# A block on one NeuronCore: the feed-forward's first product by seven block products instead of eight

## The reference, cut to what matters

```
mixed = concatenate([y_att, y_conv, y_ssd]) @ w_out            # 1024 x 1024
x = x + rms_norm_2(mixed, norm_mix_post)
h = rms_norm_2(x, norm_ffn_pre)
u = causal_dwconv(h @ ffn_w_up, ffn_conv_w) + ffn_conv_b        # 1024 x 5632, 3 taps
gate, up = split(u, 2)
x = x + rms_norm_2((silu(gate) * up) @ ffn_w_down, norm_ffn_post)
```

## Time and profile before

| | us |
|---|---|
| median of 3 runs | 3002.9 (3000.08 to 3009.09) |
| the profiled execution: its own time | 2991.82 |
| its span, first to last instruction | 2990.1 |
| PE busy | 2783.6 (93%) |
| DVE busy | 1764.5 (59%) |
| ACT busy | 1327.3 (44%) |
| POOL busy | 440.8 (15%) |
| mean granted TensorE clock | 0.968 |

### The profile page before, as it was taken

One profiled execution on the slowest core, in us unless ns is written; L12 is line 12 of the kernel. 1 busy time (PEld: TensorE's weight loads), 2 busy tenths in 40 slices (PEclk: granted clock), 3 DMA queues, 4 the chain that ended last, 5 costly groups with the idle time before them and its releaser, 6 DMA issues. The chain is left out here.

```text
span 2990.1 us, 39148 instructions
## 1 busy us (share of the span) xinstructions
PE 2783.6 (93%) x14736; PEld 2305.0 (77%) x14737; DVE 1764.5 (59%) x2288; ACT 1327.3 (44%) x1890; POOL 440.8 (15%) x389
## 2 busy tenths in 40 slices
PE   8999888989879699999996998879999999999998
PEld 7988677777768588888885876656788888888887
DVE  4441167777764599999996733856664343334313
ACT  5111255555542288787775432344553232332212
POOL 0000055554630110000001500310000000000000
PEclk9999998999989699999998999999999999999999
DMA  6446311011026399999996311010031111110114
GB/s 206 181 166 243 114 37 35 35 36 39 30 89 219 120 386 408 409 411 407 411 410 227 138 42 28 1 58 1 21 108 50 49 49 49 49 47 31 50 50 155
DMA packets 159479, 418.27 MB, mean 140 GB/s; under 512 B 21196, under 2 KB 101120, under 8 KB 146048
## 3 DMA queue, kind: packets, MB, share of 16 engines
q1 hardware_dynamic: 144752, 362.63, 32.6%
q0 software_dynamic: 8848, 33.03, 2.8%
q10 hardware_dynamic: 5760, 20.97, 1.7%
HBM read 347.92 MB, written 68.69 MB: 139 GB/s over the span
## 5 line engine op out<-in xcount | busy, mean ns | idle before, releaser
L3676 DVE SCALAR_TENSOR_TENSOR ffn_acc<-psum,ffn_taps,ffn_acc 128x1023 f32<-128x1023 f32 x88 | 112.8, 1282 | 275.7 <-ACT ffn_acc L3580 269.8
L134 PE MATMUL psum<-part,ffn_w_high 128*128 128x512 f32 x704 | 274.1, 389 | 0.7 <-DVE low L3662 0.7
L136 PE MATMUL psum<-part,ffn_w_low 128*128 128x512 f32 x704 | 273.9, 389 | 0.0
L135 PE MATMUL psum<-low,ffn_w_high 128*128 128x512 f32 x704 | 273.9, 389 | 0.0
L134 PE MATMUL psum<-part,expert_x_high 128*128 128x512 f32 x520 | 207.5, 399 | 2.9 <-issue 1.5
L136 PE MATMUL psum<-part,expert_x_low 128*128 128x512 f32 x520 | 203.7, 392 | 0.0
L134 PE MATMUL psum<-project_w_high,high 128*128 128x448 f32 (+1 forms) x512 | 194.8, 381 | 3.5 <-DVE low L398 3.5
L3580 ACT ACTIVATE ffn_acc<-psum,ffn_taps 128x1024 f32<-128x1024 f32 x44 | 53.1, 1207 | 323.2 <-PE psum L136 323.2
L135 PE MATMUL psum<-project_w_low,high 128*128 128x448 f32 (+1 forms) x512 | 193.9, 379 | 0.0
L136 PE MATMUL psum<-project_w_high,low 128*128 128x448 f32 (+1 forms) x512 | 193.8, 379 | 0.0
L129 DVE TENSOR_TENSOR expert_down_low<-expert_down,expert_down_high 128x2048 fp32r<-128x2048 f32 x62 | 139.3, 2288 | 39.6 <-ACT expert_down_high L124 39.6
(11 more groups left out here) (634 smaller groups left out, 6905.6 us busy)
## 6 DMA issues: line engine op xcount, KB each, us to landing
expert_gate<-in_w_gate_dram SPq DMA_DIRECT2D x32, 2048.0 KB
expert_up<-in_w_up_dram SPq DMA_DIRECT2D x32, 2048.0 KB, 10.0
expert_down<-in_w_down_dram SPq DMA_DIRECT2D x32, 2048.0 KB, 10.9
ffn_w<-in_ffn_w_up_dram SPq DMA_DIRECT2D x44, 512.0 KB, 3.7
y_rows<-expert_y ACTq DMA_DIRECT2D x32, 512.0 KB, 10.9
down_w<-in_ffn_w_down_dram SPq DMA_DIRECT2D x39, 256.0 KB, 2.5
project_w<-in_w_in_dram SPq DMA_DIRECT2D x4, 2048.0 KB, 11.7
mix_ret_in<-ret_feat SPq DMA_DIRECT2D x8, 1024.0 KB, 4.7
```

Source lines behind the costliest of these rows:

```text
L134: pe.matmul(out, left[0], right[0], start=start, stop=False)
L135: pe.matmul(out, left[0], right[1], start=False, stop=False)
L136: return pe.matmul(out, left[1], right[0], start=False, stop=stop)
L3676: v.scalar_tensor_tensor(out=acc[c][u][:, i:], in0=wide(psum, 4 * u + 2 * c, 2)[:, 0:S - i], scalar=taps[:, last_tap - i, ds(at, 1)], in1= ...
```

## The change

A product of 2 x 2 blocks is made with seven block products and fifteen block sums (Winograd's form) instead of eight block products. The blocks: A is the transposed weights (two feature tiles m of 128 by two halves of 512 of the width: A11, A12 of the first tile, A21, A22 of the second), B the features (two halves of the width by two halves of 512 tokens). Sums of A (S1 to S4) are made by DVE for every turn and each of gate and up, sums of B (T1 to T4) once. The seven products, their names in the code, and the PSUM bank of the four that c has: `first` A11·B11 (bank 0), `sixth` S2·T2 (1), `fifth` S1·T1 (2), `seventh` S3·T3 (3), then `third` S4·B22 (2), `fourth` A22·T4 (3), `second` A12·B21 (0). Banks 2, 3 and 0 are used twice, so DVE or ACT must have read them between: `third` waits for `u4`, `fourth` for `c22_u3`, `second` for ACT's copy of the first product (`first_copied`). `first` waits for the low part of A11 and A12 (`low_a1`), `sixth` for that of the sums (`low_sums`).

DVE's seven sums after the products are `u2`, `u4`, `c22_u3` (two), `c12`, `c21`, `c11`; their result `u` stands in SBUF, and the taps (`convolve`) read it there. `u` is one buffer for both c. `hidden` no longer fits into SBUF: each turn's two tiles are stored to DRAM and loaded again for the second product. The out-projection keeps two x tiles instead of four, its last tile interleaves the two halves (so that the transpose of tile 6 stands after 24 of its 48 matmuls), and its tail makes the T sums. Turn 0's products are written out, gate and up alternating, each waiting for its own T; turn 1 and the last are written out as well.

```diff
+            def load_after(j, c):
+
+                sp.wait_ge(made4[c], j * 2 + 2)
+                load_half(j * 2 * P + 2 * P, c, 1, second_loaded)
+                sp.wait_ge(made1[c], j * 2 + 2)
+                load_half(j * 2 * P + 2 * P, c, 0, first_loaded)
...
+            load_after(0, 0)
+            with sp.Fori(0, TURNS - 2) as j:
+                load_after(j, 1)
+                store_hidden(j)
+                load_after(j + 1, 0)
...
+            def multiply(c, b, left, right, made):
+                weights, features = room.left(c, left), room.right(right)
+                for k in range(HALF):
+                    last = three_passes(pe, bank[4 * c + b][:], [w[:, k, :] for w in weights], [f[:, k, :] for f in features],
+                                        start=(k == 0), stop=(k == HALF - 1))
+                last.then_inc(made[c], 1)
...
+            def third(j, c):
+                pe.wait_ge(combined[c], j * COMBINED + 2)
+                multiply(c, 2, "s4", "b22", made3)
+
+            def fourth(j, c):
+                pe.wait_ge(combined[c], j * COMBINED + 4)
+                multiply(c, 3, "a22", "t4", made4)
...
+            for k in range(KT):
+                if k == KT // 2:
+                    turn(TT - 2)
+                for n in range(halves):
+                    out_product(TT - 1, n, k)
...
-            step(0, 1)
-            with pe.Fori(1, TURNS) as j:
-                for u in range(2):
-                    step(j, u)
+                pe.wait_ge(combined[c], j * COMBINED)
+                first(j, c)
+                sixth(j, c)
+                fifth(j, c)
+                seventh(j, c)
+                third(j, c)
+                fourth(j, c)
+                second(j, c)
+
+            with pe.Fori(1, TURNS) as j:
+                for c in range(2):
+                    whole(j, c)
...
+                v.wait_ge(second_loaded[c], j * 16 + 16)
+                v.tensor_tensor(s1, a21, a22, ALU.add).then_inc(summed[c], 1)
+                v.wait_ge(first_loaded[c], j * 16 + 16)
+                v.wait_ge(summed[c], j * SUMS + 1)
+                v.tensor_tensor(s2, s1, a11, ALU.subtract).then_inc(summed[c], 1)
+                v.tensor_tensor(a21, a21, a11, ALU.subtract).then_inc(summed[c], 1)
+                v.wait_ge(summed[c], j * SUMS + 2)
+                v.tensor_tensor(s4, a12, s2, ALU.subtract).then_inc(summed[c], 1)
...
+            def gate_turn(j, once=False):
+                if once:
+                    sums(j, 1)
+                else:
+                    convolve(j - 1, 1, 1)
+                    convolve(j - 1, 1, 0)
+                    sums(j, 1)
+                    u2(j, 0, in_u)
+                    u4(j, 0)
+                    c22_u3(j, 0)
+                low_a1(j, 1)
+                low_a2(j, 1)
+                low_sums(j, 1)
+                hide(j - 1)
+                c12(j, 0)
+                c21(j, 0)
+                c11(j, 0, in_u)
+
+            def up_turn(j, last):
+                convolve(j, 0, 1)
+                convolve(j, 0, 0)
+                if not last:
+                    sums(j + 1, 0)
+                u2(j, 1, in_u)
+                u4(j, 1)
+                c22_u3(j, 1)
...
+                    low_a1(j + 1, 0)
+                    low_a2(j + 1, 0)
+                    low_sums(j + 1, 0)
+                c12(j, 1)
+                c21(j, 1)
+                c11(j, 1, in_u)
```

More of the change, by code:

```diff
@@ L3404, in ffn_stage @@
     with Stage(nc, "ffn") as st:
         st.adopt(out_w_loaded)
[L3406 to L3417, removed]
+        down = FfnDown(nc, st, a, bank, room, feat, store_dram, hidden_dram, out)
@@ L3513, in _ @@
                             turn(t - 1)
-                        last = three_passes(pe, out_bank(t, n)[:], (tile(low, t)[:, k, :], tile(high, t)[:, k, :]),
-                                            (half(out_w_high, n)[:, k, :], half(out_w_low, n)[:, k, :]),
-                                            start=(k == 0), stop=(k == KT - 1))
-                    last.then_inc(product, 1)
+                        out_product(t, n, k)
                 if t == 0:
@@ L3583, in gate, with take_second @@
-            def gate(j, u):
-                act.wait_ge(tapped[0][u], j * last_tap + last_tap)
-                act.activation(acc[0][u][:], acc[0][u][:], ACT.Silu).then_inc(silu_ready[u], 1)
+            def take_second(t):
+                act.wait_ge(turned, t + 1)
+                raw = late_raw if t == TT - 1 else tile(low_raw, t)[:, HALF:KT, :]
+                for k in range(HALF, KT):
+                    last = act.activation(raw[:, k - HALF, :], turned_part(k), ACT.Copy, scale=gain[:, k:k + 1])
+                last.then_inc(b22_out, 1)
@@ L3680, in hide, with t1_from @@
[L3680 to L3684 removed]
+            def t1_from(t):
+                v.wait_ge(turned, t + 1)
+                for k in range(HALF):
+                    last = v.scalar_tensor_tensor(out=tile(low_raw, t)[:, k, :], in0=turned_part(k), scalar=gain[:, k:k + 1],
+                                                  in1=tile(high, t - 4)[:, k, :], op0=ALU.mult, op1=ALU.subtract)
+                last.then_inc(t1_part, 1)
@@ new lines, in _ @@
+            add_fifth(1)
+            add_sixth(0)
+            add_second(0)
+            add_fourth(0)
+            sums(1, 0)
+            add_sixth(1)
+            low_a1(1, 0)
+            add_second(1)
+            low_a2(1, 0)
+            low_sums(1, 0)
+            add_fourth(1)
+            v.wait_ge(taps_ready, 1)
+            convolve(0, 0, 1)
+            convolve(0, 0, 0)
+            u2(1, 0, in_u)
+            u4(1, 0)
+            c22_u3(1, 0)
+            convolve(0, 1, 1, u_first[1])
@@ L3768 @@
     EARLY = 3
[L3770 to L3781 removed]
+    SOON = 2
```

671 lines of the change are left out of this document (509 added, 162 removed).

## The result

The changed kernel takes 2971.35 us (median of 4 runs, 2960.31 to 2973.98), the kernel before beside it 3001.49 (4 runs). The ratio is 0.9883, 95% interval [0.9847, 0.9920]: faster, by more than the 0.3% that can be told apart. The prediction was 2971 (2952 to 2992). In a later comparison on one chip, 6 runs against 11, the same kernel had 0.9892 [0.9870, 0.9915].

A forecast was written before the change was run, and what follows sets the result against it. PE was taken as the bound, with DVE late at single points: -59.8 + 4.1 + 1.8 + 13.7 + 6.3 + 1.7 + 1.0 - 0.8 = -32.0 us, from 2991.8 to 2960 profiled, 2971 as a median; range 2952 to 2992.

The forecast's parts named there:

- 264 matmuls, -59.8: First product: eleven turns of 168 instead of 192 matmuls, 0.2267 us each, save PE 59.8 us, the ceiling.
- Wait at the up's `third`, 8 x 0.5: Turns 2 to 9: PE waits 0.5 us for DVE's `u2` and `u4` at `third(j, 1)`, +4.1 us in all.
- that sign: Sign that the prediction is right: a turn of 38.6 us in which PE waits once, at the up's `third`.
- Tile 6, +1.8: Last out-projection tile: transpose of tile 6 after 24 matmuls instead of 36, before its input is ready; PE waits 1.8 us.
- Start, 0.9 + 6.2 + 3.3 + 3.4: Turns 0 and 1: PE waits for DVE at `fourth(0)`, `first(1, 0)`, `first(1, 1)` and `third(1, 1)`, in that order.
- Clock, 3 x 2.1: Behind the three start waits of 3.3 us or more PE's clock falls to half: +6.3 us, bounds 0 and 6.3.
- Restarts, +1.7: Each restart of PE after a wait costs 0.11 us, 15 of them: +1.7 us.
- the old wait: The kernel before had a PE wait at 2273.8 us, which goes: -0.8 us.
- Second product, +1.0: At the start of the second product PE waits for `c11` of the last turn: +1.0 us.
- DVE's load: In each turn DVE needs 34.7 us in PE's 38.1; over 90% busy from turn 2 on.
- a bound by DVE: Rival, every turn: DVE sets the time; turn 39.8 us, gain 21 (chance 0.17), or 42.2, gain nothing (0.07).
- The late loads: Rival, chance 0.06: `hidden` stores ahead of the gate's weight loads delay them; at 11 us a turn 45.6, time some 3037.

The follow-up runs named there:

- e1: Changed kernel with `u2` and `u4` ahead of the next turn's four weight sums in the up half; 2958.9 us, ratio 0.9891 against the kernel before.
- e5: Changed kernel with an unused 128x1024 DVE addition ahead of the weight sums in each up half but the last; 2989.8 us.
- e6: Changed kernel with 24, 13 and 16 additional matmuls, results overwritten, just ahead of `first(1, 0)`, `first(1, 1)` and `third(1, 1)`; 2963.8 us.
- e8: Changed kernel with each `hidden` tile stored twice, the second copy unread, in the queue ahead of the gate's loads; 2980.7 us.
- its second run: The changed kernel again, unchanged, as the measure for two other kernels; 2967.0 us, ratio 0.9892 against the kernel before.
- e2: Changed kernel with token tile 6's transpose back after 36 of the last out-projection tile's 48 matmuls; 2973.7 us.
- e4: Changed kernel with an unused 128x1024 DVE addition behind the low parts, ahead of `c12`, in each up half but the last; 2960.5 us.
- e7: Changed kernel with the sums of the up's `sixth` ahead of the weight sums that wait for turn 1's loads; 2956.8 us.
- e10: e1 with turn 1's weight sums for gate and up on GpSimd instead of DVE; 2953.2 us, ratio 0.9846 against the kernel before.

## Why the prediction was right, and where it was off

- **264 matmuls, -59.8**: 264 by the page, steps of 0.2267 as in the earlier trace rows. Right.
- **Wait at the up's `third`, 8 x 0.5**: the place is right, the size 8 x 0.81 = 6.5, a third of a us more in each. The gate's taps began 0.2 us later in the turn than I had them, since they stand behind a tile's scale on ScalarE, 1.24 us where I took 1.05; `u2` and `u4` add the rest. e1 and e5 show that this chain is the cause. The turn is 39.04 and not 38.6: this third, and the restart, which I had left out of that sign.
- **Tile 6, +1.8**: 1.81. **Start, 0.9 + 6.2 + 3.3 + 3.4**: measured 0.86, 6.02, 3.45, 4.73, in sum 15.1 for 13.7 (the terms as printed add to 13.8). The last grew though `u4` came when I had it, 87.3 us into the first product for 87.5: PE was there 1.6 us sooner (82.5 for 84.1), since `first(1, 1)` was let go 0.8 sooner than I had it and the clock behind it cost 1.46 and not 2.1. The prediction had right when that wait ends; how long it is also depends on when PE comes. (6.2 came partly out of a late landing; there DVE waited 1.93 and 1.00 us, shown above.)
- **Clock, 3 x 2.1**: it fell exactly behind the three long waits. From 2323.70 to 2326.97 eight steps took 3.27 us instead of 1.81, so 1.46 each, 4.4 in all. Other executions of the same code show 6.8 us at half instead of 3.4, so 6.3 was no bad price; what I had only named, that DVE's lateness hides some of it, is true of the second fall alone (e6). The Trainium skill (TensorE: Matmul & The Clock Gate, Part 1: The HAM clock gate) has an idle PE fall back to half of the clock, and the rows behind the three waits agree. That each wait is paid twice holds for the first and the third; the second fall is made up by a shorter wait at `third(1, 1)`.
- **Restarts, +1.7**: the terms above and the old wait give -59.8 + 15.1 + 6.5 + 4.4 - 0.8 = -34.6 for the first product; measured -33.3. The 1.3 left is about the size of the short restarts, nine at 0.11 (2561.23 to 2561.57 is 0.34).
- **Second product, +1.0**: wrong, nothing. 2724.53 to 2724.75 is a step as any other, and its first tile waits for no sum of the up half:

```profile
2724.53 0.39 PE L136 MATMUL psum<-part,ffn_w_low 128*128 128x512 f32 x1
2724.75 0.39 PE L134 MATMUL psum<-down_w_high,down_early 128*128 128x512 f32 x1
```

The rest, with `hidden` through DRAM, is 247.5 before and after.
- **DVE's load**: 33.9 us busy in a turn for my 34.7 (2521.2 to 2560.2), so that it was 86% busy in the loop and not over 90.
- **The sum**: -32.0 predicted for the stage, -31.4 measured. The profiled time fell only from 2991.8 to 2974.0, since 13.5 us more went by ahead of the stage, in the same code; the medians have 30.1. That the median came out at 2971 to within a us is luck by some us.
- **Rivals**: DVE overlaps its operations as it did (2545.15 is before 2544.01 + 1.22), so neither form of a bound by DVE came. The section of the Trainium skill that the prediction cites for it (VectorE: DVE Perf Modes, The DRAIN you can't avoid) adds that a next operation that isn't held starts earlier, so it doesn't speak against these rows. The late loads didn't come either. My 7.4 us from the issue to the use of the second load was right (7.3: 2550.60 to 2557.89), with a landing of 5.74. What the rival left out is that stores ahead of the loads also put off their issue, by 2.0 us in e8, and so narrow those 7.4 us to 5.3, less than e8's landing of 6.62.

## What to carry to other kernels

When a faster algorithm moves work from the engine that bounds to one that must work in order, list for each product the last operation that it waits for, and put what nobody waits for (here four weight sums) behind it: 6.9 us of the first product by two profiles, for a swap of two lines, at 89% load of the second engine. An added operation costs its whole step at such a point and nothing a few operations later. In a start where the second engine is late, follow its chain from wait to wait: what the first engine gains or loses counts where the second waits for it on the way (behind `first(1, 0)`), and is made up where it doesn't (behind `first(1, 1)`).

## What the runs showed of the hardware

- The granted clock fell behind some waits of 1.95 us (four of eight in e5) and 2.2 us (two of eight in e8), behind one of 2.34 that followed 16 matmuls without a use (e6), not behind one of 2.25 (e1) or those of 1.81 at tile 6, behind none of 0.8 (eight each in the changed kernel, its second run, e2, e4, e6, e7), and behind all of 3.4 or more in which PE did nothing. In some of them it had fallen before the wait was over (0.5 us before at the changed kernel's `first(1, 0)`). It stayed at half for 3.4, 6.8 or 10.2 us, for the same code at the same place 3.4 once and 6.8 once.
- A DVE operation with two operands in SBUF took 0.4 to 1.1 us more beside GpSimd additions, one with an operand in PSUM nothing; GpSimd's 128x512 addition went from 1.25 (e10, shown above) to 2.80 us.
- Two more stores of 512 KB in SyncE's queue put off the second load behind them by 2.8 us: 2.0 in its issue, 0.9 in its landing (e8).
- A 128x1536 subtraction steps by 1.67 us on DVE (2545.15 to 2546.82), midway between 1024 and 2048 as estimated.
- With identical code the part ahead of the stage took 2158.7 to 2180.7 us in 13 executions. No run here tells why.
